# Five re-ordered pieces of schedule in a hybrid encoder layer: modulation loads, last stores, gate row, last steps, first vector

## What is computed

```python
sc = jax.nn.silu(c)
mod = sc @ w_ada + b_ada                       # (1024) @ (1024, 9 * 1024)
(sh1, s1, g1, shm, smx, gm, sh2, s2, g2) = jnp.split(mod, 9, axis=-1)
h = h + 0.5 * g1 * _swiglu(_modulate(h, sh1, s1), wg1, wu1, wd1)   # wg, wu: 1024 x 2816, wd: 2816 x 1024
n = _modulate(h, shm, smx)
...                                            # conv group and attention heads, one output projection
h = h + gm * mix
h = h + 0.5 * g2 * _swiglu(_modulate(h, sh2, s2), wg2, wu2, wd2)
h = _rms(h) * g_final
```

## Time and profile before

| | us |
|---|---|
| three runs | 1993.69, 1999.65, 1997.84 |
| median | 1997.84 |
| profiled execution | 1993.16 |
| its span in the trace | 1991.4 |
| PE busy in the span | 1865.8 (94%) |
| DVE busy | 1360.5 (68%) |
| ACT busy, POOL busy | 789.0, 774.3 |

### The profile page before, as it was taken

One profiled execution on the slowest core, in us unless ns is written; L12 is line 12 of the kernel. 1 busy time (PEld: TensorE's weight loads), 2 busy tenths in 40 slices (PEclk: granted clock), 3 DMA queues, 4 the chain that ended last, 5 costly groups with the idle time before them and its releaser, 6 DMA issues.

```text
span 1991.4 us, 22690 instructions
## 1 busy us (share of the span) xinstructions
PE 1865.8 (94%) x8034; PEld 1474.6 (74%) x8034; DVE 1360.5 (68%) x1813; ACT 789.0 (40%) x1234; POOL 774.3 (39%) x604
## 2 busy tenths in 40 slices
PE   2989999999999999997999999999899999999997
PEld 2777777778788887985555555878688888878886
DVE  4777767775578786767788887247655555457778
ACT  2532222232244465226677643144232332234443
POOL 0245554555300001007999943013546555620000
PEclk7999999999999999997999998999999999999999
DMA  7054555542683352000000014122232332467333
GB/s 296 33 201 171 184 190 188 185 145 95 217 306 96 97 176 92 27 1 0 1 0 0 0 44 158 43 79 85 80 106 102 110 106 91 145 235 248 96 111 122
DMA packets 130685, 232.11 MB, mean 117 GB/s; under 512 B 8717, under 2 KB 62068, under 8 KB 130323
## 3 DMA queue, kind: packets, MB, share of 16 engines
q1 hardware_dynamic: 130578, 230.74, 33.8%
HBM read 177.75 MB, written 52.95 MB: 116 GB/s over the span
## 4 chain that ended last, share of the span: by engine, by line
PE 38%; POOL 20%; issue 18%; DVE 18%; DMA 3%; ACT 2%; SPq 0%; POOLq 0%; DVEq 0%; ACTq 0%
PE ps L821 17%; POOL sums L433 6%; PE ps L360 5%; PE ps L2448 4%; POOL HID L538 4%; PE ps L474 3%; DVE ring L451 2%; PE ps L1360 2%; PE ps L2359 2%; DVE ada_acc L975 2%; POOL base L551 2%; DVE cv L1527 2%; DMA ada_raw<-in_w_ada 1%; POOL base L556 1%; DVE negmax L1297 1%
## 5 line engine op out<-in xcount | busy, mean ns | idle before, releaser
L474 PE MATMUL ps<-T,ring 128*128 128x512 f32 x1920 | 441.9, 389 | 0.0
L474 PEld LDWEIGHTS ps<-T,ring 128*128 128x128 f32 x1920 | 360.3, 188 | 75.1 <-DVE ring L451 0.5
L474 PE MATMUL ps<-B,ring 128*128 128x512 f32 x1440 | 351.9, 401 | 6.8 <-DVE SG L531 6.8
L474 PEld LDWEIGHTS ps<-B,ring 128*128 128x128 f32 x1440 | 275.7, 192 | 75.0 <-issue 17.0
L821 PE MATMUL ps<-PW 128*128 128x512 f32 x936 | 224.8, 395 | 7.4 <-DVE PW L675 7.4
L906 POOL TENSOR_SCALAR stat<-stat 128x1 f32<-128x1 f32 x32 | 9.3, 290 | 566.4 <-ACT XS L845 271.1
L538 POOL TENSOR_TENSOR HID<-HID,SG 128x512 f32<-128x512 f32 x80 | 118.5, 1482 | 263.4 <-DVE HID L523 150.2
L821 PE MATMUL ps<-PT 128*128 128x512 f32 x912 | 214.8, 390 | 0.7 <-DVE PW L675 0.7
L821 PEld LDWEIGHTS ps<-PW 128*128 128x128 f32 x936 | 178.6, 191 | 45.8 <-DVE PW L675 8.3
L451 DVE TENSOR_TENSOR ring<-sums,ring 128x512 fp32r<-128x512 f32 x160 | 117.0, 743 | 135.4 <-ACT ring L445 135.4
L821 PEld LDWEIGHTS ps<-PT 128*128 128x128 f32 x912 | 170.8, 188 | 36.2 <-DVE PW L675 1.0
(11 more groups left out here) (297 smaller groups left out, 3253.7 us busy)
## 6 DMA issues: line engine op xcount, KB each, us to landing
adat<-ffn_hidden SPq DMA_DIRECT2D x154, 256.0 KB, 2.7
ada_raw<-in_w_ada SPq DMA_DIRECT2D x56, 512.0 KB, 3.8
rawg<-in_ffn_wg SPq DMA_DIRECT2D x21, 1024.0 KB, 5.4
ffn_hidden<-HID SPq DMA_DIRECT2D x84, 256.0 KB, 2.0
rawu<-in_ffn_wu SPq DMA_DIRECT2D x21, 1024.0 KB, 5.2
ffn_hidden<-base SPq DMA_DIRECT2D x66, 256.0 KB, 2.1
H<-in_x SPq DMA_DIRECT2D x16, 512.0 KB, 5.0
ada<-in_w_ada SPq DMA_DIRECT2D x8, 1024.0 KB, 14.0
```

The source lines that it names most:

```text
L474: mm = e.matmul(ps[:, product_bank(M, k)], ring[:, place % RING, wx, kc], RIGHT[k][:, xx, kc], start=(kc == 0 and i == 0), stop=(kc == HC ...
```

## The change

It does five things, and none changes what is computed.

1. **Pieces a group ahead.** The first two pieces of the modulation vectors of groups 2 to 7 are loaded at the end of the group before, behind the store of A11, and no longer at the start of their own group.
2. **Last stores among the left-form loads.** In each FFN, six of the seven stores of the last group (g = 10) move from the end of `sp_ffn` into `sp_down`, between the loads of the left forms of steps 4 to 8. One load of w_down moves from n = 7 to n = 10.
3. **Gate row later.** In FFN2 the gate row moves from matrix 3 to matrix 9.
4. **Last steps.** In FFN2's down product the last five steps instead of three are done tile by tile; the last two pairs have buffers of their own (`PX`), so that `act_cut` doesn't wait for PE there. PE waits for each of these steps' pairs singly, in both FFNs.
5. **Shift vector first.** At the start the loads of vector 0 are issued ahead of the first rows of x; the last piece of each of the two vectors is multiplied in two halves, and PE sums the first half while DVE makes the second. DVE's first cut of the gate weights moves behind vector 1.

```diff
-            [("_w0", [P, 2, 2, KC, P], F32R), ("PW", [P, 2, 2, 2, HALF], F32R)],
+            [("PX", [P, 2, 2, 2, HALF], F32R), ("PW", [P, 2, 2, 2, HALF], F32R)],
...
+        fs[0].tail, fs[0].more = TAIL, 0
+        fs[1].tail, fs[1].more = TAIL + 2, 2
+        ROW_M = FIRST_M + 7
...
         def act_cut(e, f, n):
             if n >= 4:
-                e.wait_ge(*f.step_mm(n - 3))
+                if n < DOWN_STEPS - f.more:
+                    e.wait_ge(*f.step_mm(n - 3))
...
-            e.wait_ge(*f.cut_lo(2 * DOWN_STEPS))
             for t in range(THALF):
-                for n in range(DOWN_STEPS - TAIL, DOWN_STEPS):
+                for n in range(DOWN_STEPS - f.tail, DOWN_STEPS):
+                    if t == 0:
+                        e.wait_ge(*f.cut_lo(2 * n + 2))
                     mm = pe_step(e, f, n, t)
...
+        def dve_ada_last(e, v, kc, src):
+            for h in range(2):
+                half = slice(h * HALF, (h + 1) * HALF)
+                if h == 0:
+                    e.wait_ge(ada_step, v * KC + kc)
+                e.scalar_tensor_tensor(out=ada_acc[:, half], in0=src[:, half], scalar=silu_c[:, kc:kc + 1], in1=ada_acc[:, half],
+                                       op0=ALU.mult, op1=ALU.add).then_inc((acc_half, ada_step)[h], 1)
         def pe_ada_sum(e, v):
-            e.wait_ge(ada_step, v * KC + KC)
+            e.wait_ge(acc_half, v + 1)
...
             for j in range(KC):
+                if j == KC // 2:
+                    e.wait_ge(ada_step, v * KC + KC)
...
-                    for kc in pieces[:2]:
+                    for kc in pieces[:2] if g == 1 or m == 1 else ():
                         sp_ada_piece(e, v, kc)
...
-                for form in (A11, A22, S3_, S1_, S2_, A12, S4_):
+                for form in (A11, A22, S3_, S1_, S2_, A12, S4_) if g + 1 < GROUPS else (A11,):
                     sp_store_hidden(e, f, g, form)
+                    if form == A11 and ada_of(f, g + 1) is not None and g > 0:
+                        for kc in range(2):
+                            sp_ada_piece(e, ada_of(f, g + 1), kc)
             e.wait_ge(*f.w_mm(product(LAST_M, K_P4)))
+        LAST_STORES = {4: (A22,), 6: (S3_, S1_), 7: (S2_, A12), 8: (S4_,)}
         def sp_down(e, f, w, rows, after):
             for n in range(4, DOWN_STEPS):
                 sp_load_left(e, f, n)
-                if n == 7:
+                for form in LAST_STORES.get(n, ()):
+                    sp_store_hidden(e, f, GROUPS - 1, form)
+                if n == 10:
...
-                    if f is fs[1] and M == FIRST_M + 1:
+                    if f is fs[1] and M == ROW_M:
...
-            for t in range(THALF):
-                e.dma_start(H[:, t], x_d[:, t]).then_inc(x_in[t], 16)
-            e.wait_ge(vec_ok, 1)
-            load_first_gu(0, 0, first_in[0].sem)
             for v in range(2):
                 for k in range(KC // 2):
                     two = slice(2 * k, 2 * k + 2)
                     e.dma_start(ada01[:, v, two], ada_d[:, two, v * D:(v + 1) * D]).then_inc(ada01_in[v][k], 16)
+                if v == 0:
+                    for t in range(THALF):
+                        e.dma_start(H[:, t], x_d[:, t]).then_inc(x_in[t], 16)
+            e.wait_ge(vec_ok, 1)
+            load_first_gu(0, 0, first_in[0].sem)
...
                 dve_ada_column(e, v)
-                if v == 0:
-                    dve_lo_gu(e, f, 0, 0, 0)
+            dve_lo_gu(e, f, 0, 0, 0)
...
+            pe_ada_sum(e, 0)
             for u in range(AHEAD):
                 pe_turn_unit(e, n, u)
-            for v in range(2):
-                pe_ada_sum(e, v)
+            pe_ada_sum(e, 1)
```

32 lines of the change are left out of this document (19 added, 13 removed).

## The result

The changed kernel takes 1964.87 us (median of four runs, 1964.48 to 1966.30); the kernel before, beside it, 1996.61 (1993.69 to 1999.65). The ratio is 0.984, with an interval of 0.9825 to 0.9859. The profiled execution of the changed kernel took 1964.48 us, its span 1962.7. The forecast was 1970.1 with a range of 1963 to 1980; the measured median lies inside that range, but under the forecast's own 1966 to 1975.

A forecast was written before the change was run, and what follows sets the result against it. PE, busy for 94% of the span, bounds the kernel, so only its gaps, low-clock stretches and the work after its end pay. Terms -5.6 - 12.0 - 4.6 + 0 + 0.3 - 5.8 = -27.7 off the 1997.84 median gave 1970.1, range 1963 to 1980.

The forecast's parts named there:

- forecast's own 1966 to 1975: Whole kernel: range of the main forecast without the rivals, given a chance of 0.68.
- what is late next: Before step 4 of FFN1's down product: DVE's two cuts end at about 540.4, just inside 540.79.
- Rival A: Start of the down products: a wait stays, step 4 late by 0.8 to 3 us per FFN; 1972 to 1977; chance 0.13.
- The charge for the clock: FFN2's matrix 3, third product: lower clock charged after a 2 us wait, 12 matmuls in about 4.3 us.
- the bounds: Part 4: -1 and +2 in FFN2 (wait costs clock), 0 to +1 in FFN1 (longer gap at the mixer costs clock).
- its own bounds: Part 5, the start: -4.5 (landing 1 us later) and -6.5 around a value of -5.8.
- B: FFN1's loop: waits reappear at piece 2 or POOL, part 1 gives 0 to -2; 1974 to 1976; chance 0.08.
- D: SP's queue: piece loads behind A11 hold SP, delaying stores and gate weights; slower only at 14 us lateness; chance 0.02.
- E: Part 5, the start: loads set the time before too, gain only PE's overlap of 1.8; 1974; chance 0.03.
- C: More than forecast: no clock lost after matrix 3's short wait, and last tiles gain; 1962 to 1966; chance 0.06.
- the bounds of the terms: Whole kernel: bounds of the unknown terms, said to add up to -17 and -33, both unlikely at once.

The follow-up runs named there:

- the dose: Changed kernel with unneeded DVE operations ahead of step 3's cut, three in FFN1 and six in FFN2: 1965.52 us in one run.
- only_tail: Kernel before with part 4 alone (last steps tile by tile, finer waits): 1997.00 us beside 1998.04, ratio 0.9993.
- order_only: Kernel before with part 5's order alone, last piece of each vector in one operation, no early PE sums: 1989.68 us, ratio 0.9959.

## Why the prediction was right, and where its steps were off

**The total.** The sum was -27.7 against the profiled execution, and the spans moved by 1991.4 - 1962.7 = 28.7. By the table that is -8.5 at the start, -5.7 in the groups, -6.6 and -5.8 at the down products and -4.7 in FFN2's products, -31.4 in all, of which the mixer gave back 2.7 (its 3.7 less the 1.0 that the finer waits had moved there). Two things that I hadn't forecast cancel: 2.7 too little for part 5, and 2.7 of luck in the mixer that the kernel before had in its profiled execution. The medians moved by 31.7, as the five places do. So taking a sum made on one execution off a median was right only if that execution was a usual one in the stretches that the change leaves alone; it lay 4.7 under the median, and I didn't ask in which stretch.

**Part 1**, forecast -5.6, measured -5.74, and -5.92 alone. Right in this execution, with its reason: no waits at pieces 0 and 1, 0.36 us at pieces 2 in all (0.20 before), and piece 6 as before (9.1 and 9.3 in all). What I didn't see is how much these waits vary: at pieces 0 and 1 they add up to 3.8 to 8.3 us in the six profiles without the part, so the part is worth that.

**Part 2**, forecast -6.4 and -5.6, measured -6.64 and -5.75. Right in size and in what is late next. The working put DVE's two cuts 1.26 us behind the end of POOL's last sum (539.14 to 540.4); the changed kernel has 1.16 in FFN1 and 0.55 in FFN2. Rival A, an instruction late by the same hold, missed by 0.3 us. What I had wrong came later, in the dose: I took the margin for DVE's own, to be used up by any work of DVE.

**Part 3**, forecast -4.6, measured -4.7. The steps too: a wait of 1.99 (forecast 2), matrix 3 by -6.88 (-6.95), matrix 9 by +2.16 (+2.35). The charge for the clock was right for this execution and isn't always: see below.

**Part 4**, forecast 0, measured 0, with the waits that the working gave, about 2 us inside the first tile, and no lower clock. The lower clock that the bounds allowed for did come in other executions with the part, behind the last wait in only_tail and at the mixer's start in three kernels; that it stayed away in the changed kernel's profile is luck.

**Part 5**, forecast -5.8, measured -8.5 in the profile. This is the step that failed, outside its own bounds. The terms: I had vector 1 done at 37.4 and PE's sum at 40.3; they came at 35.5 and 37.7. Of the 2.6 us, 1.9 are DVE's work and 0.7 PE's sum, which I took at a clock of 0.50. With the halves it began at 34.93, before the clock fell (1.00 from 30 to 35 us), and took 2.77; in order_only the same sum began at 35.41 and took 3.58. DVE's 1.9 begin with a plain slip in reading the diff: I counted the 0.5 MiB of gate weights ahead of vector 1 "in the new order as in the old", and SP asks for them behind it (16.70). At 420 GB/s that is 1.25 us, and the last pair landed at 32.15 in the trace, 1.25 before the 33.4 of the working. The other 0.6 is what I put between landing and use. I had DVE take this pair at 34.6, 1.2 behind its landing; it took it at 32.73, 0.6 behind, and only because it was still busy with the piece before. Vector 1 began at 24.70, not at 26.7, and DVE worked without a wait from 27.18 on, so its own pace, not the last landing, set the end.

**The rivals.** A, B, D and E didn't happen. The measured 1964.87 lies in the 1962 to 1966 that I gave to C with a chance of 0.06, but not for C's reasons: no clock lost in matrix 3 didn't happen in this execution (it did in four later ones), and the last tiles gained nothing. It is there by what part 5 brought beyond its bounds and by the base of the subtraction. One sum was off as well: the bounds of the terms add up to -16, not -17, at the small end.

## What to carry to other kernels

Where an engine's idle time in front of one kind of row moves the length of a loop one for one over several kernels, that row is on the path. What an edit there brings is another matter: of four further edits to these pieces, for which I expected 7 to 14 us, two brought 4.8 and 7.4 us off the loop, one 1.5, and one made it 7.5 longer. Nor is an idle stretch of DVE that waits for POOL free, since what is put there holds POOL up. When the bytes ahead of a load set a time, write down the order of the issues from the new code line by line, not from the old. And compare spans of stretches, not totals: the profiled execution is one throw, and a stretch with unchanged code tells how lucky it was.
